# Gated units: the weights keep a chunk's query columns with the four quarters innermost

## The chip, the cores and the metric

The kernel runs on one core of one Trainium2 chip. The metric is the device time of one execution in microseconds (us). The core has these engines: TensorE for matmuls (PE in the profile, with its weight loads as PEld), VectorE (DVE), ScalarE (ACT), GpSimd (POOL) and SyncE (SP, which issues DMAs).

## The reference

Two transformer blocks run one after the other on 512 tokens of width 1024 with 256 context tokens. The second block has two layers, and each mixes tokens by a short convolution, by window attention and by gated linear attention (GLA) in both directions. The change touches only the last. Cut to what matters:

```
def gla_chunk_scan(q, k, v, log_g, state0, with_output):
    ...
    b = jnp.cumsum(gc.astype(jnp.float32), axis=2)
    new_state = (jnp.exp(b_last[:, :, 0, :])[..., None] * state
                 + jnp.einsum('bhsk,bhsv->bhkv', kc * jnp.exp(b_last - b), vc))
    diff = jnp.where(lower_tri, b[:, :, :, None, :] - b[:, :, None, :, :], -jnp.inf)
    a = jnp.einsum('bhtk,bhsk,bhtsk->bhts', qc, kc, jnp.exp(diff))
    o = (jnp.einsum('bhts,bhsv->bhtv', a, vc)
         + jnp.einsum('bhtk,bhkv->bhtv', qc * jnp.exp(b), state))
```

So each query t needs a weight a[t, s] for every earlier key s of its chunk, and the output is the weights times the values, plus what the running state gives.

## The kernel before

**Units.** A layer's GLA is worked off in four units: two pairs of heads, first forward and then backward. A unit holds two heads of 64 channels in the 128 partitions, and all tokens of the layer: 768 in layer 0 (six chunks of 128), 512 in layer 1 (four chunks). `pe_gated_unit`, `act_gated_unit` and `dve_gated_unit` write out by hand what each engine does in a unit, in order. The engines meet at semaphores.

**Levels.** The weights of a chunk, P, a tile of 128 keys (partitions) by 2 heads by 128 queries a chunk, are built at seven levels with b = 64, 32, 16, 8, 4, 2, 1. At level b, a chunk falls into blocks of 2b tokens, and the queries of one half of each block get their weights for the keys of the other half. For each level VectorE subtracts a seam (line 1309), ScalarE takes exponentials (line 1206), VectorE multiplies them with queries and keys into Z (line 1423), and TensorE multiplies Z with itself (line 1163, one matmul for each chunk and head) into a PSUM slot `ps` of 128 keys by 64 queries a chunk and head.

**Writing P.** From that slot the weights go into P. At levels 64 and 32 whole blocks are valid, and ScalarE copies them (`act_put`, line 1273), one and two instructions. At levels 16 to 1 VectorE copies with a mask (`COPY_PREDICATED`, line 1454): of the 64 queries each key takes those that the byte mask `masks` names. The queries of a level lie in P as runs of b words, a run every 2b words. `masks` has 64 bytes for each direction and level.

**Output.** After the last level TensorE multiplies P with the values (line 1178) and the state with the scaled queries (line 1181), in turns by chunk. Two heads use half the array each. VectorE adds the result to `oacc` (line 1487).

**Filler.** Between the levels `between(li)` puts independent work on each engine's row: on TensorE a tile of the layer's input projection (line 490, three passes of split weights), on ScalarE and VectorE the evictions and the preparation of the next unit. Within dve_gated_unit the order is: Z of level li, the seam of level li+2, `between`, then the masked write of level li-1. So the last two masked writes (levels 2 and 1) stand behind the last Z. The first block has units of one head (`pe_unit`, `dve_unit`, lines 1111, 1128 and 1353) with `nsub == 1`; they share `act_put` and `masks`.

**Ahead of the units.** VectorE fills `blkf` (line 2562), multiplies queries and keys into Z (line 2566), TensorE sums these over each head (line 2394), and VectorE scales them into `oacc` (line 2571).

Of the kernel before, what the change touches and what calls it, by code (L numbers as in the profile page):

```python
# [22 lines left out]
U8 = mybir.dt.uint8  # L23
I32 = mybir.dt.int32

P = 128
# [5 lines left out]
CH = P  # L32
# [4 lines left out]
EPS = 1e-6  # L37
LEVELS = (64, 32, 16, 8, 4, 2, 1)
BLOCK_LEVELS = (0, 1)
RING = 4  # L40
RAW = 2
NFREQ = 8
ATT_HEADS = 8
HD = 64
# [94 lines left out]
def build(nc, ins, out):  # L139
# [4 lines left out]
    with ExitStack() as ctx:  # L144
# [7 lines left out]
        def arena(name, shape, words, dt=F32, parts=P):  # L152
            n = int(np.prod(shape)) if dt != U8 else int(np.prod(shape)) // 4
            assert words + n <= arena_words, (name, words, n, arena_words)
            return at(name, shape, A["arena"] + words, dt, parts)
# [4 lines left out]
        masks = fixed("masks", [2, 8, HD], U8)  # L160
# [94 lines left out]
        q1 = arena("q1", [4, NX], 11264)  # L255
# [16 lines left out]
        vtok2 = arena("vtok2", [ALLCH, 256], 12288)  # L272
        oacc2 = arena("oacc2", [2, NT], 13824)
        blkf = arena("blkf", [P], 18432)
        gg = arena("gg", [2, NT], 15360)
        lr = arena("lr", [NT], 16896, parts=32)
        gatew = arena("gatew", [4, P], 17664, parts=32)
# [33 lines left out]
        def mslot(s):  # L311
            return ps[:, 2 + s, :]
# [19 lines left out]
        dve_step = semaphore("dve_step")  # L332
# [84 lines left out]
        misc_free = [semaphore(f"misc_free{s}") for s in range(2)]  # L417
# [719 lines left out]
        def pe_gated_unit(pe, tally, U, vt, toks, ktok_ready, between, head, gate):  # L1137

            nch = toks // CH
            bw = U["bw"]  # L1140
            order = chunk_order(bw)

            pe.wait_ge(*ktok_ready)
            place = tally.place("misc_done")
            pe.wait_ge(misc_free[place], tally.free("misc_done"))
            m = mslot(place)
            for n_, c in enumerate(order[:5]):
                last = pe.matmul(m[:, n_ * P:(n_ + 1) * P], U["ktok"][:, c * P:(c + 1) * P], vt(c),
                                 start=True, stop=True)
            last.then_inc(misc_done, 1)  # L1150
            tally.passed("misc_done")
            for li in range(len(LEVELS)):
                pe.wait_ge(z_ready, tally.next("z_ready", 2))
                Z = U["Z"][:, li % 2, :]
                queries = halves(Z, LEVELS[li])
                place = tally.place("misc_done")
                pe.wait_ge(misc_free[place], tally.free("misc_done"))
                m = mslot(place)
                per = HD // LEVELS[li]
                for c in range(nch):  # L1160
                    for j in range(2):
                        r = slice(j * HD, (j + 1) * HD)
                        last = pe.matmul(m[:, j * NX + c * HD:j * NX + (c + 1) * HD], Z[r, c * CH:(c + 1) * CH],  # L1163
                                         queries[r, c * per:(c + 1) * per, 0 if bw else 1, :], start=True, stop=True)
                last.then_inc(misc_done, 1)
                tally.passed("misc_done")
                between(li)

            pe.wait_ge(misc_free[tally.place("misc_done", 1)], tally.read("misc_done"))
            place = tally.place("misc_done")  # L1170
            pe.wait_ge(misc_free[place], tally.free("misc_done"))
            m = mslot(place)
            for c in range(nch):
                cc = slice(c * CH, (c + 1) * CH)
                at_order = order.index(c)
                for j in range(2):
                    f = slice(j * HD, (j + 1) * HD)
                    last = pe.matmul(m[f, cc], vt(c)[:, f], U["P"][:, j, cc], start=True, stop=False,
                                     skip_group_check=True)
                    if at_order > 0:  # L1180
                        last = pe.matmul(m[f, cc], U["S"][:, at_order, f], U["eq"][:, cc], start=False, stop=True,
                                         skip_group_check=True)
            last.then_inc(misc_done, 1)
            tally.passed("misc_done")
            ktok_next = head()
            gate()
            return ktok_next
# [76 lines left out]
        def act_put(act, tally, U, li, nsub, toks, ms, done, read):  # L1264

            b, bw, nch = LEVELS[li], U["bw"], toks // CH
            act.wait_ge(misc_done, done)
            for n in range(HD // b):
                keys = slice((2 * n + bw) * b, (2 * n + bw + 1) * b)
                queries = (2 * n + 1 - bw) * b  # L1270
                dst = U["P"].rearrange("p j (c t) -> p j c t", t=CH)[keys, :, :, queries:queries + b]
                src = mslot(ms).rearrange("p (j c t) -> p j c t", j=2, t=HD)[keys, 0:nsub, 0:nch, n * b:(n + 1) * b]
                ins = act.activation(dst, src, ACT.Copy)
                if n < HD // b - 1:
                    ins.then_inc(act_step, 1)
                    act.wait_ge(act_step, tally.next("act_step"))
            ins.then_inc(misc_free[ms], 1)
            act.wait_ge(misc_free[ms], read)
# [43 lines left out]
        def dve_unit(dve, tally, U, q, k, nsub, toks, oacc, ahead, head, clear=False):  # L1322
# [18 lines left out]
            def put(li):  # L1341
                b = LEVELS[li]
                ms = tally.take("misc_done")
                dve.wait_ge(misc_done, tally.now("misc_done"))
                if li in BLOCK_LEVELS:
                    return
# [89 lines left out]
        def dve_gated_unit(dve, tally, U, q, k, toks, clear, gate, between):  # L1436

            bw = U["bw"]
            nch, nl = toks // CH, len(LEVELS)
            order = chunk_order(bw)  # L1440

            def put(li):
                b = LEVELS[li]
                ms = tally.take("misc_done")
                dve.wait_ge(misc_done, tally.now("misc_done"))
                if li in BLOCK_LEVELS:
                    return
                if li - 1 in BLOCK_LEVELS:
                    dve.wait_ge(misc_free[tally.place("misc_done", 2)], tally.read("misc_done", 2))
                dst = U["P"].rearrange("p j (c n h b) -> p j c n h b", c=nch, h=2, b=b)[:, :, :, :, 0 if bw else 1, :]  # L1450
                src = mslot(ms).rearrange("p (j t) -> p j t", j=2)[:, :, 0:toks // 2]
                src = src.rearrange("p j (c n b) -> p j c n b", c=nch, b=b)
                mk = masks[:, 1 if bw else 0, li, :].rearrange("p (n b) -> p n b", b=b).unsqueeze(1).unsqueeze(1)
                dve.copy_predicated(dst, mk.broadcast_to([P, 2, nch, HD // b, b]), src).then_inc(misc_free[ms], 1)
                dve.wait_ge(misc_free[ms], tally.read("misc_done"))

            dve_make_z(dve, tally, U, q, k, 0, toks)
            gate()
            dve_seam(dve, tally, U, 2, toks)
            dve_make_z(dve, tally, U, q, k, 1, toks)  # L1460
            dve.wait_ge(z_ready, tally.now("z_ready", -2))
            dve_seam(dve, tally, U, 3, toks)
            if clear:
                dve.memset(U["P"], 0.0).then_inc(p_clear, 1)
                dve.wait_ge(p_clear, tally.next("p_clear"))

            ms = tally.take("misc_done")
            dve.wait_ge(misc_free[ms], tally.read("misc_done"))
            for n_, c in enumerate(order[1:5]):
                dve.scalar_tensor_tensor(out=U["S"][:, n_ + 2, :], in0=U["S"][:, n_ + 1, :], scalar=U["dec"][:, c:c + 1],  # L1470
                                         in1=U["S"][:, n_ + 2, :], op0=ALU.mult, op1=ALU.add).then_inc(s_step, 1)
                dve.wait_ge(s_step, tally.next("s_step"))
            put(0)
            for li in range(2, nl):
                dve_make_z(dve, tally, U, q, k, li, toks)
                if li + 2 < nl:
                    dve.wait_ge(z_ready, tally.now("z_ready", -2))
                    dve_seam(dve, tally, U, li + 2, toks)
                between(li)
                put(li - 1)  # L1480
            put(nl - 1)
# [1042 lines left out]
        def dve_gla(dve, tally, layer, toks):  # L2524
# [7 lines left out]
            ms = tally.take("misc_done")  # L2532
# [26 lines left out]
            skip_tiles(tally, 4)  # L2559
            for back in (1, 2):  # L2560
                dve.wait_ge(slot_free[tally.place("group", back)], tally.read("group", back))
            dve.tensor_copy(blkf[:, :].rearrange("p (h f) -> p h f", h=2),
                            blk[:, :].unsqueeze(2).broadcast_to([P, 2, HD])).then_inc(dve_step, 1)
            dve.wait_ge(dve_step, tally.next("dve_step"))
# [3 lines left out]
            for t in range(2):  # L2568
                ms = tally.take("misc_done")
# [884 lines left out]
```

## Time and profile before

| | us |
|---|---|
| median of 3 runs | 3421.66 (3420.28 to 3422.48) |
| the profiled execution | 3422.17 |
| its span | 3420.1 |
| TensorE busy | 3267.6 (96%) |
| VectorE busy | 1985.5 (58%) |
| ScalarE busy | 1163.7 (34%) |

A row of the timeline has the start, the time from the first start to the last end of the instructions merged in it, the engine, line, operation, tiles (out<-in), shapes and count, and in brackets the idle time before it with what ended it. fp32 matmuls show as two instructions each. Matmuls are pipelined, so their durations overlap; their pace is read from one row's start to the next row's start. A form such as `128*64` names rows and columns of the array. The gated stretch of layer 0 is about 1742 to 1893 us, that of layer 1 about 2760 to 2889 us.

### The profile page before, as it was taken

Reading aid. Unit: us, or ns where it says so; the run is one execution under the profiler, and the core shown is the slowest. Engines: PE = TensorE matmul, PEld = TensorE weight load, DVE = VectorE, ACT = ScalarE, POOL = GpSimd, SP = SyncE. Lnnn points to the kernel's source line nnn. Section 1 sums busy time; section 2 is a strip of 40 time slices with the busy share of each in tenths; the row PEclk is TensorE's granted clock in tenths of the full one; section 3 lists DMA queues with packets and bytes.
Section 4 is the critical chain, followed back from the end, with each engine's and each line's share of the span. In section 5 each row is a group of like instructions: output and inputs, shape, how many; then the busy total and the mean of one; then the engine's idle time right before and its main releaser. Section 6 shows DMA issues by size and latency. Waiting matters only on the chain.

```text
span 3420.1 us, 49074 instructions
## 1 busy us (share of the span) xinstructions
PE 3267.6 (96%) x18400; PEld 2851.5 (83%) x18400; DVE 1985.5 (58%) x2880; ACT 1163.7 (34%) x1627; POOL 167.0 (5%) x78
## 2 busy tenths in 40 slices
PE   6999999999999999999899899999999989999998
PEld 3899999888878878887687768999999767678887
DVE  7664442748857668874569575554423467753334
ACT  3421212445531232224344363212112344633222
POOL 7100000000000000000111100000000111000000
PEclk8999999999999999999989999999999989999999
DMA  7333331321122335552111201333322211123222
GB/s 264 125 135 118 129 122 61 142 68 38 38 105 78 106 118 201 185 184 98 58 68 32 75 14 62 135 135 123 128 81 74 77 44 44 44 74 99 90 94 98
DMA packets 102045, 339.10 MB, mean 99 GB/s; under 512 B 10407, under 2 KB 21543, under 8 KB 100488
## 3 DMA queue, kind: packets, MB, share of 16 engines
q1 hardware_dynamic: 83276, 300.96, 25.3%
q10 hardware_dynamic: 18620, 36.11, 3.0%
q8 instruction: 99, 1.62, 0.2%
q14 instruction: 50, 0.41, 0.0%
HBM read 322.88 MB, written 14.16 MB: 99 GB/s over the span
## 4 chain that ended last, share of the span: by engine, by line
PE 82%; DVE 11%; ACT 4%; issue 2%; DMA 1%; ACTq 0%; POOL 0%; DVEq 0%; SPq 0%; POOLq 0%
PE ps L444 64%; PE ps L490 5%; PE ps L474 2%; PE ps L1163 1%; PE ps L2748 1%; PE ps L2183 1%; PE ps L2731 1%; PE ps L1111 1%; PE ps L2768 1%; DVE u_ex L1309 1%; PE ps L2170 1%; DVE u_Z L1423 1%; ACT wr_hi L541 1%; DVE wr_lo L551 1%; DVE xx_lo L838 1%
## 5 line engine op out<-in xcount | busy, mean ns | idle before, releaser
L541 ACT ACTIVATE wr_hi<-raw 128x1024 fp32r<-128x1024 f32 x388 | 412.4, 1063 | 591.0 <-PE ps L444 533.1
L551 DVE TENSOR_TENSOR wr_lo<-raw,wr_hi 128x1024 fp32r<-128x1024 f32 x348 | 426.3, 1225 | 81.7 <-ACT wr_hi L541 51.3
L966 DVE TENSOR_TENSOR ff_raw<-ps,ff_gate 128x768 f32<-128x768 f32 (+1 forms) x88 | 72.6, 825 | 576.0 <-PE ps L444 572.1
L444 PE MATMUL ps<-xx_hi,wr_hi 128*128 128x512 f32 x992 | 393.9, 397 | 0.7 <-ACT ff_gate L918 0.6
L444 PE MATMUL ps<-xx_lo,wr_hi 128*128 128x512 f32 x992 | 389.4, 393 | 0.0
L444 PE MATMUL ps<-xx_hi,wr_lo 128*128 128x512 f32 x992 | 389.3, 392 | 0.0
L444 PE MATMUL ps<-xa_hi,wr_hi 128*128 128x384 f32 x1344 | 341.1, 334 | 0.0
L444 PE MATMUL ps<-xa_lo,wr_hi 128*128 128x384 f32 x1344 | 340.9, 334 | 0.0
L444 PE MATMUL ps<-xa_hi,wr_lo 128*128 128x384 f32 x1344 | 340.9, 334 | 0.0
L599 DVE CUSTOM_DVE_ANT_0 ps<-raw,cb 128x1024 f32<-128x1024 f32 x240 | 295.4, 1231 | 49.7 <-DMA raw<-in_mod_stream 33.2
L444 PE MATMUL ps<-hid_hi,wr_hi 128*128 128x384 f32 (+1 forms) x1056 | 316.1, 353 | 3.8 <-DVE H L1030 2.1
L444 PE MATMUL ps<-hid_lo,wr_hi 128*128 128x384 f32 (+1 forms) x1056 | 315.6, 352 | 0.0
L444 PE MATMUL ps<-hid_hi,wr_lo 128*128 128x384 f32 (+1 forms) x1056 | 315.6, 352 | 0.0
L444 PEld LDWEIGHTS ps<-xa_hi,wr_hi 128*128 128x128 f32 x1344 | 242.5, 188 | 0.5 <-issue 0.5
L444 PEld LDWEIGHTS ps<-xa_hi,wr_lo 128*128 128x128 f32 x1344 | 242.6, 188 | 0.0
L444 PEld LDWEIGHTS ps<-xa_lo,wr_hi 128*128 128x128 f32 x1344 | 242.6, 188 | 0.0
L925 ACT ACTIVATE hid_hi<-ff_raw 128x768 f32 (+1 forms) x88 | 65.3, 742 | 508.4 <-DVE ff_raw L966 508.3
L3064 POOL TENSOR_TENSOR wr_lo<-raw,wr_hi 128x1024 fp32r<-128x1024 f32 x40 | 96.6, 2417 | 2738.4 <-ACT wr_hi L541 2738.4
L444 PEld LDWEIGHTS ps<-xx_hi,wr_hi 128*128 128x128 f32 x992 | 188.2, 190 | 43.3 <-issue 3.8
L444 PEld LDWEIGHTS ps<-xx_hi,wr_lo 128*128 128x128 f32 x992 | 187.8, 189 | 40.4
L444 PEld LDWEIGHTS ps<-xx_lo,wr_hi 128*128 128x128 f32 x992 | 187.8, 189 | 39.8 <-issue 0.8
L444 PEld LDWEIGHTS ps<-hid_hi,wr_hi 128*128 128x128 f32 x1056 | 193.2, 188 | 20.0 <-DVE hid_lo L973 2.6
(441 smaller groups left out, 5397.8 us busy)
## 6 DMA issues: line engine op xcount, KB each, us to landing
raw<-in_stream SPq DMA_DIRECT2D x392, 512.0 KB, 3.5
raw<-in_mod_stream SPq DMA_DIRECT2D x160, 512.0 KB, 4.4
hyena_k<-fst ACTq DMA_DIRECT2D x18, 256.0 KB, 5.1
hK<-hyena_k ACTq DMA_DIRECT2D x4, 1152.0 KB, 6.3
h_kept<-H ACTq DMA_DIRECT2D x2, 2048.0 KB, 9.1
cb<-in_cb ACTq DMA_DIRECT2D x3, 1024.0 KB, 5.2
H<-in_h ACTq DMA_DIRECT2D x1, 3072.0 KB, 12.9
h_kept<-H ACTq DMA_DIRECT2D x1, 3072.0 KB, 11.6
```

The source lines that it names most:

```text
L444: last = pe.matmul(gslot(slot)[:, col:col + n], w, rhs[part], start=(bi == 0 and pi == 0), stop=(bi == len(blocks) - 1 and pi == 2))
L474: last = pe.matmul(gslot(slots[t])[:, col:col + n], w, rhs[part], start=(k == 0 and pi == 0), stop=(k == steps - 1 and pi == 2))
L490: last = pe.matmul(gslot(slot)[:, col:col + n], w, rhs[part], start=(k == 0 and pi == 0), stop=(k == KC - 1 and pi == 2))
L541: act.activation(wr_hi[:, s, :], raw[:, s % RAW, :], ACT.Copy).then_inc(tile_hi, 1)
L551: dve.tensor_tensor(wr_lo[:, s, :], raw[:, s % RAW, :], wr_hi[:, s, :], ALU.subtract).then_inc(tile_lo, 1)
L599: ins = dve.tensor_tensor_reduce(out=product, in0=tile, in1=factors[:, v, :], scale=1.0, scalar=0.0, op0=ALU.mult, op1=ALU.add, accum_out= ...
L838: ins = dve.scalar_tensor_tensor(out=dst, in0=in_two(xt[:, m % 2, 0:NX]), scalar=mods[:, 8 * shift + m, 0:1], in1=high, op0=ALU.add, op1=A ...
L925: act.activation(hid[0][:, bass.ds(i * 2 + q, 1), 0:n], ff_raw[:, q:q + 1, 0:n], ACT.Copy).then_inc(hhi_ready, 1)
L966: dve.tensor_tensor(parts(ff_raw[:, q, :], with_ctx), gparts(slot, with_ctx), parts(ff_gate[:, q, :], with_ctx), ALU.mult).then_inc(slot_f ...
L1111: last = pe.matmul(m[:, j * NX + c * HD:j * NX + (c + 1) * HD], Z[r, c * CH:(c + 1) * CH], queries[r, c * per:(c + 1) * per, 0 if bw else ...
L1163: last = pe.matmul(m[:, j * NX + c * HD:j * NX + (c + 1) * HD], Z[r, c * CH:(c + 1) * CH], queries[r, c * per:(c + 1) * per, 0 if bw else ...
L3064: nc.gpsimd.tensor_tensor(wr_lo[:, s, :], raw[:, s % RAW, :], wr_hi[:, s, :], ALU.subtract).then_inc(tile_lo, 1)
```

## The change

P of the gated units gets another order of its query columns. A chunk's 128 queries are four quarters of 32. Query t of quarter hi stood in column 32*hi + t, and now it stands in column 4*t + hi. The queries of a level, runs of b words before, thus become runs of 4b words.

- The score matmuls of levels 16 to 1 read their queries with the quarters innermost, a step of 32 words between neighbouring columns. Their result in `ps` then has the order of P.
- The masked writes go to runs of 4b words. Their masks come from `masks2`, a copy of `masks` in the new order, made once for each layer by VectorE ahead of `blkf`.
- ScalarE's block writes put every word at a step of four words.
- The output matmul reads P at a step of four words, and so gets the queries back in their natural order.

The first block's units keep the old order (`nsub == 1`).

```diff
@@ pe_gated_unit @@
+                        asked = queries[r, c * per:(c + 1) * per, 0 if bw else 1, :]
+                        if li not in BLOCK_LEVELS:
+                            asked = asked.rearrange("p (hi n) b -> p n b hi", hi=QUARTERS)
                         last = pe.matmul(m[:, j * NX + c * HD:j * NX + (c + 1) * HD], Z[r, c * CH:(c + 1) * CH],
-                                         queries[r, c * per:(c + 1) * per, 0 if bw else 1, :], start=True, stop=True)
+                                         asked, start=True, stop=True)
...
-                    last = pe.matmul(m[f, cc], vt(c)[:, f], U["P"][:, j, cc], start=True, stop=False,
+                    last = pe.matmul(m[f, cc], vt(c)[:, f], U["P"][:, j, cc].rearrange("p (t hi) -> p hi t", hi=QUARTERS), start=True, stop=False,
@@ act_put @@
+                if nsub == 1:
+                    dst = U["P"].rearrange("p j (c t) -> p j c t", t=CH)[keys, :, :, queries:queries + b]
+                else:
+                    low = CH // QUARTERS
+                    q0, q1 = queries // low, (queries + b) // low
+                    dst = U["P"].rearrange("p j (c t hi) -> p j c hi t", t=low, hi=QUARTERS)[keys, :, :, q0:q1, :]
+                    src = src.rearrange("p j c (hi t) -> p j c hi t", t=low)
@@ dve_gated_unit, put @@
-                dst = U["P"].rearrange("p j (c n h b) -> p j c n h b", c=nch, h=2, b=b)[:, :, :, :, 0 if bw else 1, :]
+                run = QUARTERS * b
+                dst = U["P"].rearrange("p j (c n h b) -> p j c n h b", c=nch, h=2, b=run)[:, :, :, :, 0 if bw else 1, :]
...
-                mk = masks[:, 1 if bw else 0, li, :].rearrange("p (n b) -> p n b", b=b).unsqueeze(1).unsqueeze(1)
-                dve.copy_predicated(dst, mk.broadcast_to([P, 2, nch, HD // b, b]), src).then_inc(misc_free[ms], 1)
+                mk = masks2[:, 1 if bw else 0, li, :].rearrange("p (n b) -> p n b", b=run).unsqueeze(1).unsqueeze(1)
+                dve.copy_predicated(dst, mk.broadcast_to([P, 2, nch, HD // run, run]), src).then_inc(misc_free[ms], 1)
@@ ahead of the units, VectorE @@
+            dve.tensor_copy(masks2[:, :, :, :].rearrange("p d l (t hi) -> p (d l) t hi", hi=QUARTERS),
+                            masks[:, :, :, :].rearrange("p d l (hi t) -> p (d l) t hi", hi=QUARTERS)
+                            ).then_inc(dve_step, 1)
```

No instruction is moved past another. Two places on VectorE show what is different. The first is the end of unit 0 of layer 0, from the masked write of level 8 to the next unit's first seam; a shape's last number is the run. Before:

```order
L1454 COPY_PREDICATED u_P<-masks,ps 128x96x8
L1423 TENSOR_TENSOR u_Z<-u_ex_166,gk 128x192x2
L1423 TENSOR_TENSOR u_Z<-u_ex_166,gq 128x192x2
L1454 COPY_PREDICATED u_P<-masks,ps 128x192x4
L1423 TENSOR_TENSOR u_Z<-u_ex_164,gk 128x384
L1423 TENSOR_TENSOR u_Z<-u_ex_164,gq 128x384
L1454 COPY_PREDICATED u_P<-masks,ps 128x384x2
L1454 COPY_PREDICATED u_P<-masks,ps 128x768
L1309 TENSOR_TENSOR u_ex_164<-u_cum 128x768
```

The same place after the change, where `masks_173` is `masks2`:

```order
L1466 COPY_PREDICATED u_P<-masks_173,ps 128x24x32
L1434 TENSOR_TENSOR u_Z<-u_ex_166,gk 128x192x2
L1434 TENSOR_TENSOR u_Z<-u_ex_166,gq 128x192x2
L1466 COPY_PREDICATED u_P<-masks_173,ps 128x48x16
L1434 TENSOR_TENSOR u_Z<-u_ex_164,gk 128x384
L1434 TENSOR_TENSOR u_Z<-u_ex_164,gq 128x384
L1466 COPY_PREDICATED u_P<-masks_173,ps 128x96x8
L1466 COPY_PREDICATED u_P<-masks_173,ps 128x192x4
L1320 TENSOR_TENSOR u_ex_164<-u_cum 128x768
```

The order is the same. The four masked writes have four times the run, with the number of words kept.

The second place is ahead of the units of layer 0, again VectorE. Before:

```order
L1289 TENSOR_TENSOR u_ek<-u_cum 128x768
L882 SCALAR_TENSOR_TENSOR H<-H,vecs,rstd_88 128x512 x8
L2562 COPY blkf<-blk 128x128
L2566 TENSOR_TENSOR u_Z<-gq,gk 128x768 x2
L2571 SCALAR_TENSOR_TENSOR oacc_171<-ps,oacc_171 128x768 x2
```

After:

```order
L1300 TENSOR_TENSOR u_ek<-u_cum 128x768
L884 SCALAR_TENSOR_TENSOR H<-H,vecs,rstd_88 128x512 x8
L2574 COPY masks_173<-masks 128x1024
L2578 COPY blkf<-blk 128x128
L2582 TENSOR_TENSOR u_Z<-gq,gk 128x768 x2
L2587 SCALAR_TENSOR_TENSOR oacc_171<-ps,oacc_171 128x768 x2
```

One copy of 1024 bytes a partition is added between the residual update and `blkf`.

## Rows read from the trace of the kernel before

**Rows 1.** Page: busy time and share by engine; the chain, by engine
```profile
PE 3267.6 (96%) x18400; PEld 2851.5 (83%) x18400; DVE 1985.5 (58%) x2880; ACT 1163.7 (34%) x1627; POOL 167.0 (5%) x78
...
PE 82%; DVE 11%; ACT 4%; issue 2%; DMA 1%; ACTq 0%; POOL 0%; DVEq 0%; SPq 0%; POOLq 0%
```
**Rows 2.** Groups by form, VectorE, 1735 to 1892 us: busy, mean ns | idle before
```profile
L1454 DVE COPY_PREDICATED u_P<-masks,ps 128x768 f32<-128x768 uint8 x20 | 27.0, 1351 | 11.2 <-PE ps L1163 10.8
```
**Rows 3.** Waits of TensorE, 1735 to 1885 us: total us, times, longest
```profile
PE ps L1163 <- DVE u_Z L1423: 7.9, 6, 3.3
```
**Rows 4.** Groups by form, TensorE, whole span: the first block's output matmul
```profile
L1128 PE MATMUL ps<-u_P,vtok 128*128 128x128 f32 x64 | 12.8, 282 | 4.2 <-DVE u_P L1353 4.2
```
**Rows 5.** Timeline of VectorE: unit 1 of layer 0; two writes of layer 1
```profile
1780.97 0.56 DVE L1423 TENSOR_TENSOR u_Z<-u_ex,gk 128x384 f32<-128x384 f32 x1
...
1804.49 0.96 DVE L1454 COPY_PREDICATED u_P<-masks,ps 128x768 f32<-128x768 uint8 x1
...
1805.96 0.55 DVE L1423 TENSOR_TENSOR u_Z<-u_ex,gq 128x384 f32<-128x384 f32 x1
1806.43 1.89 DVE L1454 COPY_PREDICATED u_P<-masks,ps 128x768 f32<-128x768 uint8 x1
1810.06 1.90 DVE L1454 COPY_PREDICATED u_P<-masks,ps 128x768 f32<-128x768 uint8 x1 [1.75 <-PE ps L1163]
...
1815.98 0.96 DVE L1487 TENSOR_TENSOR oacc<-ps,oacc 128x768 f32<-128x768 f32 x1 [0.29 <-PE ps L1181]
...
2812.21 0.70 DVE L1454 COPY_PREDICATED u_P<-masks,ps 128x512 f32<-128x512 uint8 x1
...
2852.91 1.31 DVE L1454 COPY_PREDICATED u_P<-masks,ps 128x512 f32<-128x512 uint8 x1 [1.37 <-PE ps L1163]
```
**Rows 6.** The chain in order of time, unit 1: start, us, what
```profile
1787.79 0.81 ACT u_P L1273
...
1806.18 2.28 PE ps L490 x12
...
1809.95 3.32 PE ps L490 x18
```
**Rows 7.** Timeline of TensorE: end of unit 1, layer 0; output of layer 1
```profile
1804.62 1.56 PE L1163 MATMUL ps<-u_Z 64*128 64x64 f32 x24 [0.68 <-DVE u_Z L1423]
...
1813.19 0.45 PE L1178 MATMUL ps<-u_P,vtok 128*64 128x128 f32 x4
...
1813.68 0.44 PE L1178 MATMUL ps<-u_P,vtok 128*64 128x128 f32 x4
1813.90 0.44 PE L1181 MATMUL ps<-u_lf,u_S 128*64 128x128 f32 x4
...
2855.00 0.45 PE L1178 MATMUL ps<-u_P,vtok 128*64 128x128 f32 x4
```
**Rows 8.** Timeline of VectorE: the copy of blkf; the wait for the pair sums
```profile
1711.99 0.23 DVE L2562 COPY blkf<-blk 128x128 f32<-128x128 f32 x1 [2.29 <-issue]
...
1729.29 0.96 DVE L2571 SCALAR_TENSOR_TENSOR oacc<-ps,oacc 128x768 f32<-128x768 f32 x1 [13.00 <-PE ps L2394]
...
2751.08 0.69 DVE L2571 SCALAR_TENSOR_TENSOR oacc<-ps,oacc 128x512 f32<-128x512 f32 x1 [9.25 <-PE ps L2394]
```
**Rows 9.** Timeline of ScalarE: the first block write of unit 1, layer 0
```profile
1787.79 0.81 ACT L1273 ACTIVATE u_P<-ps 64x768 f32<-64x768 f32 x1
```
**Rows 10.** Timeline of TensorE: scores of 64 and outputs of 128 columns, first block
```profile
763.32 1.00 PE L1111 MATMUL ps<-u_Z 128*128 128x64 f32 x8
764.12 0.48 PE L490 MATMUL ps<-xx_hi,wr_hi 128*128 128x512 f32 x1
...
769.73 0.39 PE L1128 MATMUL ps<-u_P,vtok 128*128 128x128 f32 x2
769.95 0.39 PE L1131 MATMUL ps<-u_eq,u_S 128*128 128x128 f32 x2
```
**Rows 11.** Stretches: us, busy by engine, PEclk (granted clock), DMA share
```profile
1750.00:1778.00 28.00, 27.85 (x170) 23.82 (x172) 20.40 (x24) 8.16 (x17) 0.00 (x0) 0.51 0.02 8
```

More of the change, by code:

```diff
@@ L39 @@
 BLOCK_LEVELS = (0, 1)
+QUARTERS = 4
 RING = 4
@@ L274, in build @@
         blkf = arena("blkf", [P], 18432)
+        masks2 = arena("masks2", [2, 8, HD], 18560, U8)
         gg = arena("gg", [2, NT], 15360)
@@ L1270, in act_put @@
                 queries = (2 * n + 1 - bw) * b
-                dst = U["P"].rearrange("p j (c t) -> p j c t", t=CH)[keys, :, :, queries:queries + b]
                 src = mslot(ms).rearrange("p (j c t) -> p j c t", j=2, t=HD)[keys, 0:nsub, 0:nch, n * b:(n + 1) * b]
+                if nsub == 1:
[5 more added lines that the diff above has]
+                    src = src.rearrange("p j c (hi t) -> p j c hi t", t=low)
                 ins = act.activation(dst, src, ACT.Copy)
@@ L1449, in put @@
                     dve.wait_ge(misc_free[tally.place("misc_done", 2)], tally.read("misc_done", 2))
-                dst = U["P"].rearrange("p j (c n h b) -> p j c n h b", c=nch, h=2, b=b)[:, :, :, :, 0 if bw else 1, :]
+                run = QUARTERS * b
+                dst = U["P"].rearrange("p j (c n h b) -> p j c n h b", c=nch, h=2, b=run)[:, :, :, :, 0 if bw else 1, :]
                 src = mslot(ms).rearrange("p (j t) -> p j t", j=2)[:, :, 0:toks // 2]
-                src = src.rearrange("p j (c n b) -> p j c n b", c=nch, b=b)
-                mk = masks[:, 1 if bw else 0, li, :].rearrange("p (n b) -> p n b", b=b).unsqueeze(1).unsqueeze(1)
-                dve.copy_predicated(dst, mk.broadcast_to([P, 2, nch, HD // b, b]), src).then_inc(misc_free[ms], 1)
+                src = src.rearrange("p j (c n b) -> p j c n b", c=nch, b=run)
+                mk = masks2[:, 1 if bw else 0, li, :].rearrange("p (n b) -> p n b", b=run).unsqueeze(1).unsqueeze(1)
+                dve.copy_predicated(dst, mk.broadcast_to([P, 2, nch, HD // run, run]), src).then_inc(misc_free[ms], 1)
                 dve.wait_ge(misc_free[ms], tally.read("misc_done"))
@@ L2561, in dve_gla @@
                 dve.wait_ge(slot_free[tally.place("group", back)], tally.read("group", back))
+            dve.tensor_copy(masks2[:, :, :, :].rearrange("p d l (t hi) -> p (d l) t hi", hi=QUARTERS),
+                            masks[:, :, :, :].rearrange("p d l (hi t) -> p (d l) t hi", hi=QUARTERS)
+                            ).then_inc(dve_step, 1)
+            dve.wait_ge(dve_step, tally.next("dve_step"))
             dve.tensor_copy(blkf[:, :].rearrange("p (h f) -> p h f", h=2),
```

## The prediction, made before the changed kernel was run

> **What bounds the kernel now.** I read the page first. TensorE is busy for 96% of the span, the chain of waits lies on it for 82%, and VectorE carries 11% of the chain [rows 1]. So a shorter VectorE instruction helps only where TensorE stands still for it. Next came the groups of instructions of the gated stretch of layer 0 (1735 to 1892 us), where the 20 masked writes cost 27.0 us of VectorE. In the idle time before them VectorE waits 10.8 us for TensorE; TensorE does not wait for them [rows 2]. TensorE's own waits in that stretch say the same: the longest row is 7.9 us for the products Z, two smaller ones are for ScalarE's copy of the keys and for the output sum, and none is for a masked write [rows 3]. The one place where TensorE does wait for a masked write, 4.2 us in all, is line 1353. That is the first block's unit, whose layout the change leaves as it is [rows 4].
>
> Then the stretch by time, for unit 1 of layer 0. Its masked writes take 0.96 us for runs of 4 words, 1.89 for runs of 2 and 1.90 for runs of 1 [rows 5]. The coarser ones are as fast as the first: with 8 of the 20 at 1.89 us, the other 12 share 27.0 - 15.1 = 11.9 us, 0.99 us each [rows 2]. So only the last two of a unit are slow, and the last Z product (1805.96) is issued ahead of both. What remains for TensorE after it is the scores of the last level, 18 matmuls of filler on line 490 (3.32 us on the chain), and only then the output matmul on line 1178 at 1813.19 [rows 6, 7]. The last masked write runs from 1810.06 to 1811.96. It is done 1.23 us before it is wanted. The same distance (end of the last write against the first start on line 1178) is positive in all eight units, between 0.8 and 2.3 us. The narrowest is 2852.91 + 1.31 = 2854.22 against 2855.00 [rows 5, 7].
>
> **The change part by part.**
>
> Masked writes. Levels of runs 16, 8, 4, 2, 1 become runs 64, 32, 16, 8, 4. Runs of 4 and more are the fast rows already: 0.96 to 0.99 us for 768 elements, 0.70 us for 512 [rows 2, 5]. So I take 1.0 and 0.70 us for all. Saved on VectorE: in layer 0, 8 instructions by 0.89 us = 7.1 us; in layer 1, 8 by (1.31 - 0.70) = 4.9 us; 12.0 us together. On the path: nothing. The cover is the filler on line 490, and the distances above are all positive already. If that cover were gone, the value would be up to 1.9 us a unit.
>
> What comes next after an earlier last write: VectorE runs the next unit's head (the seams, the decay products) and then waits 0.29 us for TensorE's output before the sum at 1815.98 [rows 5]. That sum is released by TensorE already. An earlier head lengthens this wait and moves nothing. Gain 0.
>
> The new mask copy. One copy of 1024 bytes a partition for each layer, ahead of the copy of `blkf`. The nearest rows are 0.23 us for 128 elements and 1.9 us for a slow masked write of 768 elements [rows 5, 8]; scaled to 1024 that is between 0.3 and 2.5 us. The products behind it are released earlier by that much less, and VectorE then idles 13.00 us in layer 0 and 9.25 us in layer 1, until TensorE has worked through filler and delivers the pair sums [rows 8]. Taken as 0; without that cover it would cost 0.6 to 5 us in all.
>
> ScalarE's block writes (levels 64 and 32) now write every fourth word: one instruction of 64x768, 0.81 us when it writes contiguously [rows 9], and two half as wide. The trace has no ScalarE write with such a step. Lower bound: unchanged, since the unmasked Z products take 0.56 and 0.55 us at runs of 64 and of 1 word alike [rows 5]. Upper bound: what short runs cost VectorE's masked write, 0.89 us for 768 elements. The first of them is on the chain in units 1 and 3 (unit 1's row stands in [rows 6]); with layer 1 counted alike that is at most 2 by 0.89 + 2 by 0.60 = 3.0 us. I take 0, by the nearer row: it has no mask either.
>
> TensorE's reads are the uncertain term. The output matmul's moving operand is now read at a step of four words (16 bytes), the score matmuls of five levels at a step of 32 words. Neither step occurs in the trace; score matmuls from level 64 to level 1 (a step of two words) take 1.55 to 1.56 us for 24 [rows 7]. But those are covered: eight instructions of 64 columns advance 0.80 us (0.10 each) at line 1111, while two of 128 columns advance 0.22 us (0.11 each) at line 1128 [rows 10]. Half the columns, nearly the same pace. So a score matmul waits for its weights, not its columns, and a read twice as slow would just fit. The output matmul has no such room. Four instructions of 128 columns and half the array each advance 0.22 us, two side by side [rows 7]. There are 160, thus 80 pairs of 0.11 us. Twice as slow is 80 by 0.11 = 8.8 us, all on the chain. Bounds: 0 and 8.8 us for line 1178 (17.6 us at a third of the pace), 0 for the scores unless slower than half. A gain is excluded, since no read becomes denser. I take 0. These fp32 matmuls take 0.11 us for 128 columns, while the filler of line 490 takes 2.28 us for 12 matmuls of 4608 columns together [rows 6], so 0.06 us for 128. An fp32 pass asks for a word only about half as often as the stream that the memory feeds there, which leaves slack for a sparser read.
>
> The Trainium skill says otherwise at first sight: "Advanced Engine Details and Errata", section "SBUF Cachelines", has lines of 16 bytes and a penalty when each access goes to a different line, with two hits needed to hide the latency. By that rule every word at a step of 16 bytes pays; the sum would be the 8.8 us above instead of 0, which is rival B. The trace does not settle it, since its widest step still has two words to a line. For masked writes the trace is stricter than the page: runs of two words, two hits to a line, take 1.89 us against 0.96 us [rows 5].
>
> The sum, against the profiled execution: 3422.17 us (span 3420.1) + 0 + 0 + 0 + 0 = 3422 us. The median of the runs is 3421.66, half a microsecond off.
>
> **The rivals.** A measurement of this kernel can tell a difference of about 0.2% (6.8 us) from none.
>
> A, the forecast: all savings lie under filler, reads at a step are free. 3422 us, from 3419 to 3424. With ScalarE's upper bound (A2) 3425 us.
>
> B, slower: TensorE reads the output matmul's operand at half pace. For it: a step to a new 16-byte stretch for every word, which the kernel has nowhere now, and the chain passes through line 1178 in every unit. Against it: the fp32 pass is slow itself. 3422 + 8.8 = 3431 us. It decides once a 128-column instruction needs more than 0.11 us a pair.
>
> C, much slower: the step of 32 words hurts the score matmuls too, at a third of the pace. 800 instructions, 400 pairs; a pair's columns would take 0.165 instead of the 0.11 us that its weights take, + 22 us, of which about half is hidden where TensorE waits for Z anyway; with 17.6 us for the output matmuls 3422 + 17.6 + 11 = 3451 us.
>
> D, faster: the freed VectorE time counts. For it: the chain does run through VectorE in parts of units 1 to 3. Against it: the slow masked writes stand behind the last Z, under filler [rows 5, 6]. If it all counted: 3422 - 12.0 = 3410 us. A milder form of it is a shorter stretch at the low clock: the granted clock is 0.51 from 1750 to 1778 us [rows 11], and shortening such a stretch by a few us is worth as much.
>
> E, the writes do not become fast since it is the small level, not the run, that costs. Then 3422 us as well; the time cannot tell it from A, the rows can.
>
> **How the numbers follow.** A 0.56, A2 0.06, E 0.02 (same, 0.64); B 0.22 and C 0.04 (slower, 0.26); D 0.10 (faster). The likeliest is A, 3422 us. The range leaves out C and most of D: it reaches up past B (3431) and down to a D that is worth some microseconds, 3416 to 3432. Same-sign cases hold most of the chance, so A's own range, 3419 to 3424, stands only for the case that every read is free.
>
> **What would show it.** All 40 masked writes of the gated units at 0.70 to 1.02 us; the idle time before the output sum up by about 1.8 us in unit 1, with its start unchanged against the matmul; line 1178's pairs still 0.11 us apart (A) or 0.22 us (B); 24 score matmuls in 1.55 us (A, B) or over 2 us (C); ScalarE's block write at 0.81 us (A) or up to 1.7 us (A2). The forecast is wrong if line 1178's pace changes, or if TensorE's waits for Z shrink.

## The result, and the profile after

The changed kernel takes 3437.74 us (median of 5, 3434.29 to 3442.63) against 3420.28 us (median of 5, 3416.51 to 3422.48): a ratio of 1.0051, 95% interval 1.004 to 1.0062. It is slower by 17.5 us, where no change was forecast. The time lies above the forecast range (3416 to 3432). The profiled execution took 3442.63 us with a span of 3440.5, so it is 20.5 us above that of before (3422.17), and it is the longest of the five. Shares worked out from the two traces refer to these 20 us. The ratios are worked out over all runs and are not always the quotient of the two medians; where the two differ by a microsecond or more, both are given.

Line numbers move: 490 is now 492, 1163 is 1168, 1178 is 1183, 1181 is 1186, 1273 is 1284, 1298 (the subtraction that ends the preparation of the next unit) is 1309, 1309 (the seam) is 1320, 1423 is 1434, 1454 is 1466 and 1487 is 1499. In the kernels of the experiments they can move by some lines more, so rows are best compared by their tiles.

**What was meant to get faster did.** The timeline of VectorE in unit 1 of layer 0, where the columns are start, duration, engine, line, operation, tiles, shapes, and in brackets the idle time before it with its releaser (compare [rows 5]):

```profile
1802.21 3.15 DVE L1309 TENSOR_TENSOR u_cum<-u_ktok,u_ek 128x768 f32<-128x768 f32 x1
1805.39 1.01 DVE L1466 COPY_PREDICATED u_P<-masks,ps 128x768 f32<-128x768 uint8 x1
...
1809.54 1.00 DVE L1466 COPY_PREDICATED u_P<-masks,ps 128x768 f32<-128x768 uint8 x1
1814.58 0.97 DVE L1466 COPY_PREDICATED u_P<-masks,ps 128x768 f32<-128x768 uint8 x1 [4.04 <-PE ps L1168]
...
1821.95 0.96 DVE L1499 TENSOR_TENSOR oacc<-ps,oacc 128x768 f32<-128x768 f32 x1 [2.67 <-PE ps L1186]
```

The masked writes of levels 2 and 1 (1809.54, 1814.58) went from 1.89 and 1.90 us to 1.00 and 0.97. The saving went into idle time: VectorE now waits 4.04 us instead of 1.75 before the last write, and 2.67 instead of 0.29 before the sum. The first row is new: a subtraction that took 0.96 us before stands for 3.15.

**What got slower: ScalarE's block writes.** The timeline of ScalarE, same unit (compare [rows 9]):

```profile
1788.77 1.56 ACT L1284 ACTIVATE u_P<-ps 64x768 f32<-64x768 f32 x1
...
1793.97 1.80 ACT L1284 ACTIVATE u_P<-ps 32x384 f32<-32x384 f32 x2
```

**And TensorE's output matmul.** The timeline of TensorE, same unit (compare [rows 7]):

```profile
1817.77 0.66 PE L1183 MATMUL ps<-u_P,vtok 128*64 128x128 f32 x4
1818.24 0.42 PE L1186 MATMUL ps<-u_lf,u_S 128*64 128x128 f32 x4
1818.47 0.66 PE L1183 MATMUL ps<-u_P,vtok 128*64 128x128 f32 x4
1818.91 0.44 PE L1186 MATMUL ps<-u_lf,u_S 128*64 128x128 f32 x4
1819.15 0.66 PE L1183 MATMUL ps<-u_P,vtok 128*64 128x128 f32 x4
```

From one start to the next, the four instructions that read P at a step of four words advance 0.44 us (1818.47 to 1818.91). The four beside them, which read contiguously, advance 0.24 us (1818.91 to 1819.15). Before, both took 0.22.

**TensorE waits longer for Z, and its clock falls more often.** The waits of TensorE in the stretch of layer 0 (1735 to 1910 us), then stretches around the ends of units 1 and 2 (columns: length, busy of PE, PEld, DVE, ACT, POOL, granted clock, DMA share, GB/s):

```profile
PE ps L1168 <- DVE u_Z L1434: 11.3, 6, 3.3
```

```profile
1805.00:1823.00 18.00, 15.18 (x129) 12.79 (x129) 10.98 (x15) 4.03 (x8) 0.00 (x0) 0.91 0.09 30
1845.00:1862.00 17.00, 14.45 (x103) 12.12 (x103) 11.15 (x13) 3.50 (x7) 0.84 (x1) 0.80 0.10 32
```

The same stretches of before:

```profile
1802.00:1817.00 15.00, 14.00 (x141) 11.89 (x139) 12.79 (x14) 4.13 (x9) 1.68 (x1) 1.00 0.11 36
1838.00:1853.00 15.00, 14.05 (x140) 12.08 (x139) 12.80 (x13) 4.13 (x8) 2.18 (x1) 1.00 0.11 36
```

The wait grew from 7.9 to 11.3 us [rows 3]. Where the clock stood at its full 2.4 GHz in both stretches, after the longer waits part of each runs at 1.2 GHz. At the end of unit 3 the granted clock was 0.91 already before, and is now 0.80.

**Where the 20 us come from, by comparing the starts of the same instructions in both traces.** From the first seam of layer 0 (1729) to the last sum (1892) the changed kernel falls 14.7 us behind: 5.3 us while the output matmuls run (1.1 in unit 0, 1.4 in each other), 1.3 us behind ScalarE's first block write in units 1 and 2 (0.74 and 0.55), 2.3 us where the subtraction takes 3.15 us (1.13 in each of units 1 and 2), and 5.7 us between the last Z and the output matmul, where more of TensorE's work runs at the low clock. Layer 1 adds 4.5 us, 3.6 of it in the output matmuls. The remaining 1.3 us arise outside the two stretches, in code that is the same in both kernels: 1.6 us are lost between the layers where the clock was low for longer, and some tenths come back elsewhere. I count them as variation between executions.

### The profile page after: what moved, and what is told of

It reads as the page before. It is cut to its first block, busy times and chain, and to the rows that moved or that the text cites. A ratio compares the mean times of both kernels' runs of the same rounds, so it can differ in the third digit from the quotient of the medians.

```text
span 3440.5 us, 49076 instructions
## 1 busy us (share of the span) xinstructions
PE 3281.9 (95%) x18400; PEld 2858.9 (83%) x18400; DVE 1977.2 (57%) x2882; ACT 1171.5 (34%) x1627; POOL 166.9 (5%) x78
## 4 chain that ended last, share of the span: by engine, by line
PE 82%; DVE 11%; ACT 4%; issue 2%; DMA 1%; ACTq 0%; POOL 0%; DVEq 0%; SPq 0%; POOLq 0%
PE ps L446 63%; PE ps L492 5%; PE ps L476 2%; PE ps L1168 1%; PE ps L2764 1%; PE ps L2195 1%; PE ps L2747 1%; PE ps L1113 1%; PE ps L2784 1%; DVE u_ex L1320 1%; PE ps L2182 1%; DVE u_Z L1434 1%; ACT wr_hi L543 1%; PE ps L1183 1%; PE ps L2423 1%
## 6 DMA issues: line engine op xcount, KB each, us to landing
h_kept<-H ACTq DMA_DIRECT2D x1, 3072.0 KB, 11.3
```

## The experiments

Theory: the loss has two sources, each a step of four words on a path that has no cover. TensorE reads at half pace (8.8 us), and ScalarE writes at half pace, and ScalarE's delay costs more than itself, by what it moves. Rivals: the step on the score matmuls costs as well; the saving on VectorE counts and was outweighed; the low clock is chance.

**The change with the output matmul reading contiguously.**

```diff
-U["P"][:, j, cc].rearrange("p (t hi) -> p hi t", hi=QUARTERS), start=True, stop=False,
+U["P"][:, j, cc], start=True, stop=False,
```

> The changed kernel, but the output matmul of the gated units reads P contiguously again (so the output has its queries in the wrong order: P itself is still built in the new order). Theory: the step of four words costs this matmul 0.22 us for four instructions, 8.8 us in all, the largest of three terms. Expected: four instructions of line 1183 advance 0.22 us instead of 0.46; the time is 8 to 10 us below the changed kernel, 3428 to 3430 us, ratio to before about 1.002 to 1.003. Rival (the loss comes from ScalarE's writes and what they set off, the matmul's slower pace being filled elsewhere): at most 3 us back, ratio 1.004 or more.

Measured: 3431.18 us, ratio 1.0032 (1.002 to 1.0044). Four instructions advance 0.22 us again. The timeline of TensorE of this kernel:

```profile
1819.98 0.44 PE L1183 MATMUL ps<-u_P,vtok 128*64 128x128 f32 x4
1820.20 0.44 PE L1186 MATMUL ps<-u_lf,u_S 128*64 128x128 f32 x4
```

It gives back 1.0051 - 1.0032 = 0.0019, 6.5 us: less than the 8 to 10 expected, but the interval covers them. It covers the rival's 1.004 as well; the same step on the kernel before (below) is what decides between them.

**The change with contiguous block writes.** In `act_put` the branch of one-head units is taken always.

```diff
-                if nsub == 1:
+                if True:
```

> The changed kernel, but ScalarE writes the blocks of levels 64 and 32 contiguously as before (so these weights stand in wrong columns). Theory: the writes go back from 1.55 to 0.81 us and from 0.88 to 0.48 us; directly on the chain that is about 2 us, but the earlier ScalarE also moves the split of weights on GpSimd (line 3080), behind which VectorE's line 1309 stood for 2.2 us in units 1 and 2 of layer 0, and shortens TensorE's wait and the low clock after it. Expected: 5 to 9 us below the changed kernel, ratio to before 1.0025 to 1.0035. Rival (only the direct cost counts, the low clock is chance): 2 us back, ratio 1.0045.

Measured: 3432.50 us, ratio 1.0036 (1.0023 to 1.0048): 5.2 us back, at the low end of the 5 to 9 expected. The wait for Z is 7.7 us again, and in unit 1 the subtraction takes its usual time. By the traces the direct cost is 1.3 us in layer 0, so more than that came back. The rival's 1.0045 is still inside the interval; the two experiments with ScalarE's writes together decide it (below).

**Both undone.**

> The changed kernel with both undone: contiguous read of P by the output matmul and contiguous block writes (the result is wrong in the order of columns). What is left of the change: masked writes with runs of 4 words and more, scores with a step of 32 words, the mask copy. Theory: the masked writes' saving of 12 us on VectorE lies under filler, so this is within 0.15% of before, 3417 to 3424 us. Rival (the saving does count, and was only outweighed): 3408 to 3412 us, ratio 0.997. Second rival (the score matmuls' step costs too): 3425 us or more.

Measured: 3421.29 us (12 runs), ratio 1.0004 (0.9995 to 1.0012). The masked writes are fast here as well, 40 of them, 11.5 us less of VectorE (34.5 us against 46.0), and nothing of it reaches the time. This is the cleanest test of the forecast's central claim, and it holds. The rival at 0.997 is excluded; the second rival, at 1.0015, lies just outside too. Undone one at a time, the two sources gave back 6.5 and 5.2 us, together they give back 16. The 4 us between lie within the uncertainty of these intervals, so whether the two reinforce each other is not shown.

**The kernel before with the strided read alone.** The same edit in reverse, on line 1178 with `hi=4`.

> The kernel before, with one line changed: the output matmul of the gated units reads P at a step of four words (the result is wrong in the order of columns). Theory: +8.8 us, ratio 1.0026, and four instructions of line 1178 advance 0.46 us instead of 0.22. Rival (the matmul is slower only in the changed kernel, for another reason such as a late VectorE or ScalarE): no difference.

Measured: 3428.51 us, ratio 1.0023 (1.0013 to 1.0034), 7.9 us (8.9 us between the medians). The timeline of TensorE:

```profile
1820.76 0.66 PE L1178 MATMUL ps<-u_P,vtok 128*64 128x128 f32 x4
1821.19 0.44 PE L1181 MATMUL ps<-u_lf,u_S 128*64 128x128 f32 x4
```

0.43 us for four (0.43 to 0.47 over the whole output), with nothing else of the change in place. So the read is the cause.

**Two and eight words.** The same line with `hi=2` and `hi=8`, for what kind of step costs.

> The kernel before, with the output matmul reading P at a step of two words, two in every 16 bytes (wrong columns). Theory (what costs is a new 16-byte stretch for every word): no cost, four instructions of line 1178 advance 0.22 us, ratio 0.9995 to 1.0005. Rival (any step costs): somewhere up to the 0.46 us of step four.

> The kernel before, with the output matmul reading P at a step of eight words (wrong columns). Theory: as at four words, 0.46 us for four instructions, ratio 1.0023 to 1.0028. Rival (the cost grows with the step, as with a miss that lies farther away): above 0.6 us and a ratio over 1.004.

Measured: step 2: 3422.64 us, 1.0005 (0.9995 to 1.0014). Step 8: 3431.40 us, 1.0027 (1.0017 to 1.0038), 9.2 us (10.6 between the medians). The timeline of TensorE, at step two:

```profile
1816.54 0.46 PE L1178 MATMUL ps<-u_P,vtok 128*64 128x128 f32 x4
1816.77 0.45 PE L1181 MATMUL ps<-u_lf,u_S 128*64 128x128 f32 x4
```

and at step eight:

```profile
1816.67 0.66 PE L1178 MATMUL ps<-u_P,vtok 128*64 128x128 f32 x4
1817.11 0.44 PE L1181 MATMUL ps<-u_lf,u_S 128*64 128x128 f32 x4
```

The pace is 0.22 us contiguous, 0.23 at two words, 0.43 at four, 0.44 at eight. The cost is a stair between two and four words (a step of three was not run), as the Trainium skill has it in "Advanced Engine Details and Errata", section "SBUF Cachelines": lines of 16 bytes, two hits to a line are enough, one is not. Here it is a factor of two, and no more at a step of eight.

**The scores' step alone.** On the kernel before, line 1163 gets the operand `asked` of the diff for levels 16 to 1, with nothing else changed.

> The kernel before, with only the score matmuls of levels 16 to 1 reading their queries at a step of 32 words (wrong columns). Theory: their columns fit under the weight load even at half pace, so 24 of them take 1.28 to 1.34 us from first to last start instead of 1.28; at most 1 us in all, ratio 0.9995 to 1.0005. Rival (the step costs as much as the output matmul's): 24 take over 2 us, ratio 1.003 or more.

Measured: 3422.38 us, ratio 1.0006 (0.9997 to 1.0015). In the timeline of TensorE a score group of level 32 and the one of level 16, the first strided level, read:

```profile
1787.66 1.55 PE L1166 MATMUL ps<-u_Z 64*128 64x64 f32 x24
1791.46 1.62 PE L1166 MATMUL ps<-u_Z 64*128 64x64 f32 x24
```

0.07 us for 24. The step costs only what does not fit beside the weight load, which is nearly nothing, as the forecast had it. Where the clock was low, the groups take 2.83 us with and without the step. There are 40 strided groups, 20 of 24 matmuls and 20 of 16 (which take 1.17 instead of 1.11 us), so the whole comes to 2.6 us at most. The ratio lies a hair above the expected 1.0005, which its interval covers.

**ScalarE's writes alone.** On the kernel before, `act_put` writes at a step of four words.

```diff
-                dst = U["P"].rearrange("p j (c t) -> p j c t", t=CH)[keys, :, :, queries:queries + b]
+                    dst = U["P"].rearrange("p j (c t hi) -> p j c hi t", t=low, hi=4)[keys, :, :, q0:q1, :]
```

> The kernel before, with only ScalarE's block writes of the gated units put at a step of four words (wrong columns). Theory: the first write takes 1.55 instead of 0.81 us; ScalarE's split of the next weights comes a microsecond later, GpSimd's part with it, and VectorE's line 1298 then stands beside it for 3.1 instead of 0.96 us in units 1 and 2 of layer 0, while the following Z (line 1423) no longer takes 1.6 us. Expected: TensorE's wait for Z in the stretch of layer 0 from 7.9 to about 11.4 us, ratio to before 1.0015 to 1.003 (5 to 10 us). Rival (only the direct cost of about 2 us): ratio below 1.001.

Measured: 3431.55 us (11 runs), ratio 1.0023 (1.0014 to 1.0032), 7.9 us (10.8 us between the medians, which is the upper end of the interval). The rival (below 1.001) is excluded. The three timelines side by side, ScalarE, GpSimd, VectorE:

```profile
1788.62 1.56 ACT L1279 ACTIVATE u_P<-ps 64x768 f32<-64x768 f32 x1
...
1800.84 1.06 ACT L541 ACTIVATE wr_hi<-raw 128x1024 fp32r<-128x1024 f32 x1
```

```profile
1801.98 2.40 POOL L3070 TENSOR_TENSOR wr_lo<-raw,wr_hi 128x1024 fp32r<-128x1024 f32 x1 [11.86 <-ACT wr_hi L541]
```

```profile
1802.04 3.15 DVE L1304 TENSOR_TENSOR u_cum<-u_ktok,u_ek 128x768 f32<-128x768 f32 x1
1805.22 0.99 DVE L1460 COPY_PREDICATED u_P<-masks,ps 128x768 f32<-128x768 uint8 x1
```

GpSimd splits weights as soon as ScalarE has made their high part. It starts at 1801.98 and ends at 1804.38. VectorE's subtraction, issued 0.06 us later with both inputs in SBUF, ends at 1805.19: 0.8 us after GpSimd, as if it had started then. In the kernel before the split ran from 1801.15 to 1803.68. It then fell beside a masked write, which reads PSUM and was not held (1.01 us), and held only the Z product behind it, for one microsecond (1.60 instead of 0.56 us). GpSimd's row, then VectorE's:

```profile
1801.15 2.53 POOL L3064 TENSOR_TENSOR wr_lo<-raw,wr_hi 128x1024 fp32r<-128x1024 f32 x1 [11.88 <-ACT wr_hi L541]
1800.45 0.96 DVE L1298 TENSOR_TENSOR u_cum<-u_ktok,u_ek 128x768 f32<-128x768 f32 x1
1801.45 1.01 DVE L1454 COPY_PREDICATED u_P<-masks,ps 128x768 f32<-128x768 uint8 x1
1802.49 1.60 DVE L1423 TENSOR_TENSOR u_Z<-u_ex,gk 128x384 f32<-128x384 f32 x1
```

What moved against the split is VectorE. Counted from the start of the first block write (1787.79 before, 1788.62 here), GpSimd's split starts after 13.36 us in both kernels, so it did not come later, as I had expected. VectorE's subtraction starts after 13.42 instead of 12.66 us. VectorE is late because one of its Z products needs exponentials (`u_ex`) that ScalarE makes behind the block write. Its wait for them, before and here:

```profile
1791.89 0.56 DVE L1423 TENSOR_TENSOR u_Z<-u_ex,gk 128x384 f32<-128x384 f32 x1 [0.16 <-ACT u_ex L1206]
```

```profile
1793.48 0.56 DVE L1429 TENSOR_TENSOR u_Z<-u_ex,gk 128x384 f32<-128x384 f32 x1 [0.89 <-ACT u_ex L1206]
```

So 0.75 us of ScalarE is followed by 1.1 us more of collision (2.19 us lost instead of 1.05), and then by a longer wait of TensorE and a stretch at the low clock. The wait for Z is 11.5 us here, 7.9 before. "SBUF — State Buffer", section "Who interferes with whom" in the Trainium skill, bears on it: a VectorE instruction with two SBUF inputs contends with a GpSimd instruction that reads SBUF, over a pair of ports that is locked and not shared out. The rows agree: the subtraction stood for all of the split's 2.40 us.

The starts of the same instructions, compared as above, bear the two sources out in layer 0. From the first seam to the last sum this kernel falls 9.4 us behind the kernel before, and the kernel with the strided read alone 5.1 us; together 14.5, and the change lost 14.7. In layer 1 this trace is no witness: this kernel gains 4.5 us there, but so do the kernel with both undone (3.9 us) and the one with a step of two words (4.1 us), which have none of ScalarE's strided writes. Layer 1 thus differs by some 4 us from trace to trace, for a reason other than these writes, which stays open.

**Without GpSimd's splits.** To price the collision by itself, GpSimd computes 8 of 1024 words of each split in the second block, on both kernels. The low parts of these weights keep old values otherwise.

```diff
-                        nc.gpsimd.tensor_tensor(wr_lo[:, s, :], raw[:, s % RAW, :], wr_hi[:, s, :],
+                        nc.gpsimd.tensor_tensor(wr_lo[:, s, 0:8], raw[:, s % RAW, 0:8], wr_hi[:, s, 0:8],
```

> The kernel before, with GpSimd's splits in the second block (line 3064) cut from 1024 to 8 words a partition, so that nearly nothing runs beside VectorE (the low parts of these weights keep old values). Theory (VectorE's long instructions, 1.6 us on line 1423 and 2.1 us and more on others, are its SBUF operands standing behind GpSimd): they go back to 0.55 and 0.96 us. How much of it is on the chain: a few us, ratio 0.997 to 0.9995. Rival (they are long for another reason): the long rows stay and the ratio is 1.000.

> The changed kernel with the same cut of GpSimd's splits. Theory: VectorE's line 1309 goes from 3.15 to 0.96 us in units 1 and 2, so this gains at least 2 us more than the same cut gains on the kernel before: the difference between the two cut kernels is 13 to 16 us instead of 17.5. What remains of it is 8.8 us of output matmuls, 2 to 3 us of ScalarE's writes and low clock. Rival (the collision with GpSimd does not matter for the change): 17 us or more apart.

Measured: before without splits 3405.93 us, 0.9944 (0.993 to 0.9957); changed without splits 3417.13 us, 0.9982 (0.9972 to 0.9991). The timeline of VectorE on the kernel before without splits, then on the changed one:

```profile
1803.40 0.56 DVE L1423 TENSOR_TENSOR u_Z<-u_ex,gk 128x384 f32<-128x384 f32 x1
```

```profile
1806.03 0.97 DVE L1309 TENSOR_TENSOR u_cum<-u_ktok,u_ek 128x768 f32<-128x768 f32 x1
```

Both long rows are gone. So is a third that the change never touched, four updates of the state in unit 1; before, and before without splits:

```profile
1786.31 3.50 DVE L1470 SCALAR_TENSOR_TENSOR u_S<-u_S,dec 128x128 f32<-128x128 f32 x4
```

```profile
1787.24 1.51 DVE L1470 SCALAR_TENSOR_TENSOR u_S<-u_S,dec 128x128 f32<-128x128 f32 x4
```

The kernel before gains 16.6 us of median (the kernel before beside it took 3422.53 us), well beyond the 2 to 10 us expected. The collision is a cost of its own in the tuned kernel. The two kernels are 11.2 us apart by the medians, 13 by the ratios (13 to 16 were expected), instead of 17.5: so the distance shrinks by about 5 us, with some 4 us of uncertainty on that difference. That is not quite the collision's share. Without the splits TensorE waits for ScalarE's block writes themselves, for 1.0 us in layer 0 and 4.6 us in layer 1 of the changed kernel (none and 2.2 us in the kernel before; with the splits none and 0.5 in the changed one), so their own delay weighs more there.

**GpSimd's split in four pieces: a version that beats both.** If VectorE stands behind one GpSimd instruction, shorter ones let it in between. Nothing is left out here.

```diff
-                        nc.gpsimd.tensor_tensor(wr_lo[:, s, :], raw[:, s % RAW, :], wr_hi[:, s, :],
-                                                ALU.subtract).then_inc(tile_lo, 1)
+                        for piece in range(4):
+                            part = slice(piece * D // 4, (piece + 1) * D // 4)
+                            done = nc.gpsimd.tensor_tensor(wr_lo[:, s, part], raw[:, s % RAW, part], wr_hi[:, s, part],
+                                                           ALU.subtract)
+                        done.then_inc(tile_lo, 1)
```

> The kernel before with each of GpSimd's splits in the second block (line 3064) issued as four instructions of 256 words instead of one of 1024; nothing is left out. Theory: VectorE stands behind one GpSimd instruction, not behind the whole split, so its stalls of up to 2.2 us fall to 0.6 to 1.2 us; the cut of nearly the whole split gave 0.9944, and this gives a part of that: ratio 0.996 to 0.999. Rival (VectorE waits for all of GpSimd's queued work, or four instructions cost more than they free): 1.000 or slower.

> The changed kernel with the same four pieces. Theory: the collision on line 1309 falls from 2.2 us to about 1 us, so the distance to the kernel before with the same pieces lies between the 12 to 13 us measured without GpSimd's splits and the 17.5 us of the change: ratio to before 0.9995 to 1.003. Rival: 1.005 as the change itself.

Measured: the kernel before in pieces 3409.32 us, ratio 0.9964 (0.995 to 0.9978); the changed one in pieces 3427.59 us, 1.0022 (1.0011 to 1.0033). The first is the fastest complete kernel of this study, some 12 us below the kernel before. The timelines of VectorE and GpSimd of the first:

```profile
1798.73 1.02 DVE L1454 COPY_PREDICATED u_P<-masks,ps 128x768 f32<-128x768 uint8 x1
1799.78 0.63 DVE L1423 TENSOR_TENSOR u_Z<-u_ex,gk 128x384 f32<-128x384 f32 x1
1800.33 1.09 DVE L1423 TENSOR_TENSOR u_Z<-u_ex,gq 128x384 f32<-128x384 f32 x1
```

```profile
1798.45 3.56 POOL L3066 TENSOR_TENSOR wr_lo<-raw,wr_hi 128x256 fp32r<-128x256 f32 x4 [11.02 <-ACT wr_hi L541]
```

The stalls fall to 0.1 and 0.5 us, and the split takes 3.56 instead of 2.53 us. Four pieces take 2.8 to 2.9 us in half of the 40 splits of this trace, so part of that is the price of four instructions; the rest, I take it, is GpSimd giving way in its turn. One thing went against my expectation. The changed kernel gained in proportion less than I expected for it: its own ratio lies in the expected range, but its distance to the kernel before with the same pieces is 18.3 us (19.8 by the ratios), not 12 to 17.5, though its subtraction fell from 3.15 to 1.50 us. With ratios known to about 0.1% each, the two distances cannot be told apart, so pieces do not prove that the change's own share of the collision disappears.

## Why the prediction was wrong, step by step

**Masked writes: right, in rows and time.** All 40 take 0.70 to 1.04 us (forecast 0.70 to 1.02), 11.5 us less in all (forecast 12.0). The saving lies under filler, as the kernel with both sources undone shows (1.0004).

**The mask copy: right.** It takes 1.16 us (between the bounds 0.3 and 2.5), and the wait behind it shrank from 13.00 to 11.87 us. It also moved a collision, which went unforeseen: GpSimd's split (1713.01 to 1715.40) now meets the small copy of `blkf`, 0.23 us before [rows 8], and no longer the two Z products behind it, which took 4.03 us and now take 1.83. (In the changed kernel without the splits, the copy takes 0.23 us again.) The timeline of VectorE after the change:

```profile
1711.92 1.16 DVE L2574 COPY masks<-masks 128x1024 uint8<-128x1024 uint8 x1 [2.31 <-issue]
1713.11 2.37 DVE L2578 COPY blkf<-blk 128x128 f32<-128x128 f32 x1
```

**TensorE's output read: the wrong value taken, both ends right.** Bounds 0 and 8.8 us; measured 7.9 us alone, 8.9 by the traces (5.3 + 3.6). The failing step is the argument that an fp32 pass asks for a word only half as often and so leaves slack. I had no row at a step over two words, so the low end had no support, and I preferred an argument worked out from pace to the rule quoted right beside it. By the rule, rival B (3431 us) would have been the forecast. The prediction had named a change of line 1178's pace as a sign that it is wrong, and that sign came; TensorE's waits for Z, its other sign, grew instead of shrinking.

**The score matmuls: right.** 0.07 us for 24, hidden by the weight load.

**ScalarE's writes: the term that was mis-sized.** I took 0 us "by the nearer row", an unmasked VectorE write with a step of two words. But that row has two words in each 16 bytes. The write at four words took 1.56 instead of 0.81 us, by 0.75 us, near the upper bound of 0.89. The upper bound for the sum, 3.0 us, was wrong as well: it counted only ScalarE's own delay. Alone the writes cost 7.9 us. I had not asked who waits for a later ScalarE: VectorE does, for its exponentials, and it then falls beside a GpSimd split that it had missed before. The row that would have warned me lay at hand, the Z product of 1.60 us in unit 1 among others of 0.56.

**The rivals.** B and the ScalarE bound A2 were treated as alternatives, 0.22 and 0.06. They come from one thing, the step of four words that the new layout puts on both engines, so they come together: A2 and B made 3422 + 8.8 + 3.0 = 3434 us even with my own prices, above the range. With the prices measured one at a time, the sum is 7.9 + 7.9 = 15.8 us, or 18.4 us with the at most 2.6 of the scores, and 17.5 was measured. By ratios, 1.0023 + 0.0023 + 0.0006 is 1.0052 against 1.0051. Each of these ratios is known to about 0.001 (3.4 us), so that they meet this closely is partly luck; the gaps between the medians (8.9, 10.8 and 1.6 us) add up to 21.3.

**Still open.** How the 7.9 us of ScalarE's writes divide into delay, collision and low clock is read from the traces, not measured apart. The granted clock was held fixed in no run, and its share of 5.7 us in layer 0 is an attribution. What layer 1 adds comes from one execution of each kernel, and traces differ there by some 4 us for a reason that I have not found.

## What to carry to other kernels

A layout that makes one engine's writes dense makes other engines' accesses sparse: list every reader and writer of the tile, and look for each for a row at its new step. Here TensorE's read was free at a step of two words and took twice as long at four, while VectorE's masked write was slow already at runs of two. Two alternatives with the same cause are one case, and their prices add. And an engine that is delayed by less than a microsecond moves all that starts behind it: look for instructions of one form with two durations, they show what already collides, and may be worth more than the change at hand.

## What the runs showed of the hardware

- TensorE's moving operand in fp32, 128 columns on half the array: 0.22 us for four instructions contiguously, 0.23 at a step of two words, 0.43 at four, 0.44 at eight.
- ScalarE's write in fp32 at a step of four words: 1.56 instead of 0.81 us for 768 elements.
- VectorE's masked write: 0.96 to 1.04 us with runs of four words and more, 1.9 with one or two. The unmasked product shows no such cost at a step of two words (0.55 us).
- A VectorE subtraction with both inputs in SBUF, issued 0.06 us behind a GpSimd subtraction of 2.40 us, took 3.15 instead of 0.96 us; a masked write from PSUM beside one took its usual 1.01 us. A copy from SBUF to SBUF of 128 words, issued 0.10 us behind a GpSimd subtraction, took 2.37 instead of 0.23 us. Cutting GpSimd's instructions into four made the kernel before 0.36% faster (0.2 to 0.5%).
